# Storing the attention keys from the feature-major tile element by element, in place of turning them to token rows on TensorE

## The chip, the cores and the metric

One core of a Trainium2 chip runs the whole step in one launch. The time is that of the device, in microseconds (us); lower is better. The kernel before has a median of 3550.0 us over 2 runs (3547.46 and 3552.54).

## The reference, cut to what matters

The step pushes two groups of tokens through two layers: a prompt of 16 + 512 = 528 tokens and a sample of 32 tokens, 560 columns in all. Layer 0 is a gated DeltaNet. After it one shared set of keys, values and forget gates is made, and layer 1 is a forgetting attention with 16 heads of 128 features, over the prompt's own keys and, for the sample, over 1024 cached keys and its own 32. The part that the change touches is this:

```
k = rms_norm((rms_norm(h, kv_norm_g) @ kv_w)[..., :2048].reshape(B, L, 16, 128), k_norm_g)
...
return (y_prompt, y_sample, ..., k_p (1, 528, 16, 128), v_p, logf_p, ..., k_s (1, 32, 16, 128), v_s, logf_s)
```

The normed keys are used in the attention and are outputs too: `k_p` and `k_s` are laid out by token, then head, then feature, in float32. The 128 features of one token and head are 512 bytes in a row; the next token's row of the same head lies 16 * 128 * 4 = 8192 bytes further.

## The kernel before, in words

Three stages run one after the other: the DeltaNet layer (up to about 2200 us), the attention layer (`attention_layer`) and an output layer. Activations are kept feature-major: a tile has 128 features on the partitions and the 560 tokens along the free dimension. In the attention stage a **turn** handles two heads at once: in front, the projections of head p (four tiles: key, value, query, gate; each of 2 x 8 `kstep`s of six 280-column matmuls, L1860), and behind them the attention of head p - 1. There are 17 turns: turn 0 has only the front, turns 1 to 15 have both, and the last turn (16) has the last head's attention beside a part of the output projection.

What stands where in a turn is written out by hand in `HEAD_PLACES` (L1602) and `LAST_HEAD_PLACES`: each step has a place among the 64 ksteps, and every engine walks the same list and runs its own part of each step in that order. A step that waits holds up all that stands behind it on its engine. The steps that matter here, with their places:

- `tab` at 2.01: VectorE writes the head's normed keys `kT` and queries `qT` (L2207), both [128 features, 560 tokens], and then `fq`. These three raise `kq_made`. There is one `kT`, so `tab` of the next turn overwrites it, and L2205 makes VectorE wait until the key transposes of the turn before are done (`k_turned`).
- `score` 0 at 11.01: TensorE's first matmul of the attention; it waits for `kq_made`. The splits that make each weight half tile ready (VectorE L2137 and L2142, ScalarE L1988) stand between these steps; `split` at 2.02 is just behind `tab`. TensorE can be two half tiles (16 ksteps) ahead of them.
- `kout` at 64.01, the turn's end: TensorE turns `kT` to token rows with six transposes into the PSUM tiles `b_E` (L1899, L1902), ScalarE copies them to `kn` and `kn2` (L2047, L2049) and issues three stores on its DMA queue (L2053 to L2055). In the last turn `kout` stands at 2.01.
- `put` at 64.03: ScalarE stores the head's attention output `fo` on the same queue.

SyncE loads the weight halves (L1821) into a ring of four. At the end of the stage ScalarE waits for all key and value stores (L2098, L2099).

Other transfers that the rows below name, with the length of one contiguous run: `cl_rows` (L1441) and `wf` (L1439) are loaded in runs of 16 float32, 64 bytes, 1024 and 2048 of them; `TTs` (L780) in 1280 runs of 128 bytes; `M` (L762) is stored in DRAM in 320 runs of 128 bytes an issue; `GT` in 32 runs of 2560 bytes; the log gates (L2011, L2012) in 512 and in 16 runs of 64 bytes; weight halves in 1024 runs of 512 bytes.

Of the kernel before, what the change touches and what calls it, by code (L numbers as in the profile page):

```python
# [22 lines left out]
P = 128  # L23
# [4 lines left out]
PROMPT = N_META + SEQ  # L28
SAMPLE = 32
NTOK = PROMPT + SAMPLE  # L30
# [25 lines left out]
FH = 16  # L56
# [138 lines left out]
def wait(engine, point):  # L195

    if point is not None:
        engine.wait_ge(*point)
# [1480 lines left out]
def attention_layer(nc, top, io, keep, scratch):  # L1679
# [4 lines left out]
    with ExitStack() as ctx:  # L1684
        def sb(name, shape, dt=F32):
            return ctx.enter_context(nc.sbuf_tensor("b_" + name, shape, dt))
# [4 lines left out]
        def signal(name, kind, per=1):  # L1691
            return Signal(sem(name), kind, per)

        main = [ctx.enter_context(nc.psum_tensor(f"b_main{i}", [P, 512], F32)) for i in range(4)]
        E = [ctx.enter_context(nc.psum_tensor(f"b_E{i}", [P, 512], F32)) for i in range(2)]
        F = keep["F"]
# [4 lines left out]
        raw = sb("raw", [P, 3, NTOK])  # L1701
        sq, root, rr = sb("sq", [P, NTOK]), sb("root", [P, NTOK]), sb("rr", [P, 2, NTOK])
        kT, qT = sb("kT", [P, NTOK]), sb("qT", [P, NTOK])
        zt, znew, zs = sb("zt", [P, NTOK]), sb("znew", [P, NTOK]), sb("zs", [P, NTOK])
        kn, vn = sb("kn", [P, 4, P]), sb("vn", [P, 4, P])
        kn2, vn2 = sb("kn2", [SAMPLE, 2, P]), sb("vn2", [SAMPLE, 2, P])
        kc, vc = sb("kc", [P, PAST // P, P]), sb("vc", [P, PAST // P, P])
        kcT = sb("kcT", [P, PAST])
        fbp, fbs = sb("fbp", [P, PROMPT]), sb("fbs", [SAMPLE, PAST + SAMPLE])
# [20 lines left out]
        sumsq = signal("sumsq", "sumsq")  # L1730
        rooted, inverted = signal("rooted", "root"), signal("inverted", "recip")
        moved = signal("moved", "tab")
        kq_made = signal("kq_made", "tab", 3)
        k_turned, k_took, k_out = signal("k_turned", "kout"), signal("k_took", "kout"), signal("k_out", "kout", 48)
        v_turned, v_took, v_out = signal("v_turned", "vout"), signal("v_took", "vout"), signal("v_out", "vout", 48)
        kc_in, vc_in = signal("kc_in", "fetchk", 16), signal("vc_in", "fetch", 16)
        fb_in = signal("fb_in", "fetch", 32)
        kc_turned, kc_took = signal("kc_turned", "kcache"), signal("kc_took", "kcache")
# [5 lines left out]
        fo_out = signal("fo_out", "put", 16)  # L1744

        bank_e = [
            Bank({"kout": (lambda: True, k_took), "kcache": (lambda: True, kc_took), "sumsq": (lambda t: True, rooted),
                  "turn": (lambda i: True, pt_made)}),
            Bank({"kout": (lambda: True, k_took), "kcache": (lambda: True, kc_took), "sumsq": (lambda t: True, rooted),
                  "value": (lambda i: True, gated), "score": (lambda i: i == 5, biased)}),  # L1750
        ]
        bank_f = [
            Bank({"vout": (lambda: True, v_took), "score": (lambda i: i % 2 == 0 or i >= 4, biased)}),
            Bank({"vout": (lambda: True, v_took), "score": (lambda i: i % 2 == 1 or i >= 4, biased)}),
        ]
# [70 lines left out]
        def _(pe):  # L1826

            def body(turn):
                p = turn.p
                for step in turn.steps():  # L1830
# [18 lines left out]
                    elif what == "kstep":  # L1849
                        n, k = a  # L1850
                        t = n // 2
# [14 lines left out]
                    elif what == "gates":  # L1866
# [10 lines left out]
                        elif n == 4:  # L1877
                            pe.wait_ge(g_v, 7)
                            for i in range(BLOCKS):
                                nc.tensor.transpose(E[0][0:QN[i], FH * i:FH * i + FH], lf[3][:, Q0[i]:Q0[i] + QN[i]], ident[0:FH, 0:FH])  # L1880
                                src = fp[:, Q0[i]:Q0[i] + QN[i]] if i < 5 else fs[:, PAST:PAST + SAMPLE]
                                m = nc.tensor.transpose(E[1][0:QN[i], FH * i:FH * i + FH], src, ident[0:FH, 0:FH])
                            m.then_inc(g_p, 1)
                    elif what == "sumsq":
                        t, = a
# [4 lines left out]
                            wait(pe, bank_e[e].free(turn, step))  # L1890
                            m = nc.tensor.matmul(E[e][:, 0:HALF], ones[:, :], sq[:, e * HALF:(e + 1) * HALF], start=True, stop=True)
                        m.then_inc(sumsq.sem, 1)
                    elif what in ("kout", "vout"):
                        src, b, guards, sig = ((kT[:], E, bank_e, k_turned) if what == "kout" else (raw[:, 1], F, bank_f, v_turned))
                        wait(pe, kq_made.after(turn))
                        for g in guards:
                            wait(pe, g.free(turn, step))
# [23 lines left out]
                    elif what == "turn":  # L1921
# [4 lines left out]
                        for j in range(nb):  # L1926
                            n = tail if j == nb - 1 else P
                            out, src = E[0][0:n, QN[i] * j:QN[i] * j + QN[i]], pr[0:QN[i], i % 2, P * j:P * j + n]
# [27 lines left out]
        def _(act):  # L1956
            kp, ks = (io[n].rearrange("b t h d -> (b t) h d") for n in ("k_p", "k_s"))
            vp, vs = (io[n].rearrange("b t h d -> (b t) h d") for n in ("v_p", "v_s"))
            cache_k, cache_v = (io[n].rearrange("b (c p) h d -> p (b c) h d", p=P) for n in ("cache_k", "cache_v"))

            def body(turn):
                p = turn.p
                again = not (turn.fixed and p == 1)
                for step in turn.steps():
                    what, *a = step
                    if what == "o_split":
                        k, = a
                        if k < FH - 1:
                            act.wait_ge(o_in[k % O_RING], 16 * (k // O_RING + 1))
                            src = o_raw[:, k % O_RING]  # L1970
                        else:
                            wait(act, gated.after(turn, 5))
                            src = fo[:]
# [40 lines left out]
                    elif what == "evac":  # L2014
                        t, = a
# [10 lines left out]
                    elif what == "root":  # L2026
                        t, = a
# [6 lines left out]
                    elif what == "tab":  # L2034
# [1 line left out]
                            wait(act, gated.after(turn, 5, ago=1))  # L2036
                        wait(act, gate.after(turn, ago=1))
                        nc.scalar.activation(zs[:], znew[:], ACT.Copy).then_inc(moved.sem, 1)
                    elif what in ("kout", "vout"):
                        turned, took, out, b, rows, rows2, dst, dst2 = (  # L2040
                            (k_turned, k_took, k_out, E, kn, kn2, kp, ks) if what == "kout" else
                            (v_turned, v_took, v_out, F, vn, vn2, vp, vs))
                        wait(act, turned.after(turn))
                        if again:
                            wait(act, out.after(turn, ago=1))
# [6 lines left out]
                        h = bass.ds(p - 1, 1)  # L2052
# [42 lines left out]
                        wait(act, gated.after(turn, 5))  # L2095
                        act.dma_start(scratch["fo"][bass.ds(p - 1, 1)].rearrange("k p t -> p (k t)"), fo[:]).then_inc(fo_out.sem, 16)
            turns(act, body)
            act.wait_ge(k_out.sem, 48 * FH)  # L2098
            act.wait_ge(v_out.sem, 48 * FH)  # L2099
            act.wait_ge(fo_out.sem, 16 * (FH - 1))  # L2100
            act.wait_ge(stored, 5 * 16)
# [2 lines left out]
        def _(dve):  # L2104
            def body(turn):
                p = turn.p
                again = not (turn.fixed and p == 1)
                for step in turn.steps():
# [68 lines left out]
                    elif what == "evac":  # L2177
                        t, = a
                        dve.wait_ge(sub_used, SUBS_B * p + 2 * t + 2)
                        b = main[2 * (t % 2):2 * (t % 2) + 2]  # L2180
# [4 lines left out]
                        out = znew if t == 3 else raw[:, t]  # L2185
# [15 lines left out]
                    elif what == "tab":  # L2201
                        wait(dve, inverted.after(turn, 2, 1, ago=1))
                        if again:
                            wait(dve, scored.after(turn, 5, ago=1))
                            wait(dve, k_turned.after(turn, ago=1))  # L2205
                        for out, t, g in ((kT, 0, 49), (qT, 2, 50)):
                            nc.vector.scalar_tensor_tensor(out=out[:], in0=raw[:, t], scalar=vec[:, g:g + 1], in1=rr[:, t // 2],  # L2207
                                                           op0=ALU.mult, op1=ALU.mult).then_inc(kq_made.sem, 1)
# [239 lines left out]
```

## Time and profile before

| | |
|---|---|
| median of 2 runs | 3550.0 us |
| profiled execution, its own time | 3539.89 us |
| its span, first to last instruction | 3538.0 us |
| mean granted TensorE clock | 0.976 |
| TensorE matmuls busy | 3393.7 us (96%) |
| VectorE / ScalarE busy | 2160.1 us (61%) / 1466.1 us (41%) |
| DMA packets, bytes | 689799, 375.75 MB |

A row of the page gives, for one engine, the busy time and its share of the span; the digits show the span in 40 slices of 88 us. Rows of the timeline give start, length, engine, line, what is written and read, and in brackets the idle time ahead of it with what ended it.

### The profile page before, as it was taken

The page shows a single profiled execution, that of the slowest core. Times are in us where ns is not written, and L with a number is a line of the kernel's source. Part 1 is how long each engine was busy: PE and PEld are TensorE (multiplying, and loading weights), DVE is VectorE, ACT ScalarE, POOL GpSimd, SP SyncE. Part 2 cuts the span into 40 slices and gives each one's busy share as a digit, 9 for nine tenths or more (in the row PEclk, how much of TensorE's full clock was granted, in tenths as well). Part 3 has the DMA queues.
Part 4 walks back from the last instruction along what each step waited for, and adds up shares of the span by engine and source line. Part 5 has one row for each costly group of instructions (what it writes and reads, how often), then busy time and mean ns, then how long its engine had stood idle before and what let it go on. Part 6 is the DMA issues. An engine that isn't in the chain of part 4 may idle for free. (4 is left out here: it accounts for less than half of the span.)

```text
span 3538.0 us, 68787 instructions
## 1 busy us (share of the span) xinstructions
PE 3393.7 (96%) x25217; PEld 3249.8 (92%) x25217; DVE 2160.1 (61%) x3614; ACT 1466.1 (41%) x3062; POOL 794.1 (22%) x1058
## 2 busy tenths in 40 slices
PE   4989999999999999999889999999999999999799
PEld 2989999999999999999889998999899999999799
DVE  5656766777766767767533234766666666666522
ACT  4345545555555555555422222333333333333312
POOL 2333555544444555344400000000000000000000
PEclk7999999999999999999899999999999999999999
DMA  4423344343433343333545433333333333333343
GB/s 145 107 73 98 107 104 115 92 109 80 111 104 98 104 115 90 89 101 98 152 121 164 129 118 101 98 98 97 97 85 103 88 97 96 96 97 107 115 136 111
DMA packets 689799, 375.75 MB, mean 106 GB/s; under 512 B 135443, under 2 KB 654470, under 8 KB 689126
## 3 DMA queue, kind: packets, MB, share of 16 engines
q1 hardware_dynamic: 591958, 303.36, 31.6%
q10 hardware_dynamic: 97728, 70.81, 6.7%
q8 instruction: 80, 1.31, 0.2%
q14 instruction: 33, 0.27, 0.0%
HBM read 297.98 MB, written 55.15 MB: 100 GB/s over the span
## 5 line engine op out<-in xcount | busy, mean ns | idle before, releaser
L933 PE MATMUL main<-xh,w_hi 128*128 128x280 f32 x3072 | 712.5, 313 | 14.2 <-DVE w_lo L1206 14.2
L933 PE MATMUL main<-xh,w_lo 128*128 128x280 f32 x3072 | 651.6, 293 | 0.0
L933 PE MATMUL main<-xl,w_hi 128*128 128x280 f32 x3072 | 648.9, 293 | 0.0
L933 PEld LDWEIGHTS main<-xh,w_hi 128*128 128x128 f32 x3072 | 496.5, 191 | 26.4 <-issue 15.1
L933 PEld LDWEIGHTS main<-xh,w_lo 128*128 128x128 f32 x3072 | 493.0, 190 | 0.0
L933 PEld LDWEIGHTS main<-xl,w_hi 128*128 128x128 f32 x3072 | 490.8, 190 | 0.0
L1860 PE MATMUL b_main<-xh,w_hi 128*128 128x280 f32 x2048 | 471.6, 312 | 0.0
L1860 PE MATMUL b_main<-xh,w_lo 128*128 128x280 f32 x2048 | 432.2, 292 | 0.0
L1860 PE MATMUL b_main<-xl,w_hi 128*128 128x280 f32 x2048 | 431.6, 292 | 0.0
L888 POOL TENSOR_TENSOR prod<-Ml,Tl 40x30 f32<-40x30 f32 (+14 forms) x480 | 330.1, 688 | 37.6
L1860 PEld LDWEIGHTS b_main<-xh,w_hi 128*128 128x128 f32 x2048 | 326.0, 190 | 12.0
L892 POOL TENSOR_TENSOR Tl<-Tl,prod 40x30 f32<-40x30 f32 (+14 forms) x480 | 324.1, 675 | 37.6
L1860 PEld LDWEIGHTS b_main<-xh,w_lo 128*128 128x128 f32 x2048 | 327.3, 190 | 0.0
L1860 PEld LDWEIGHTS b_main<-xl,w_hi 128*128 128x128 f32 x2048 | 326.1, 189 | 0.0
L1206 DVE TENSOR_TENSOR w_lo<-w_raw,w_hi 128x1024 fp32r<-128x1024 f32 x192 | 249.3, 1298 | 62.6 <-ACT w_hi L1053 61.1
L1215 DVE SCALAR_TENSOR_TENSOR y<-xp,cw,y 128x640 f32<-128x640 f32 x192 | 195.3, 1017 | 106.2 <-ACT y L1073 92.0
L2142 DVE TENSOR_TENSOR w_lo<-b_w_raw,w_hi 128x1024 fp32r<-128x1024 f32 x126 | 153.3, 1216 | 136.1 <-ACT w_hi L1988 136.1
L1137 ACT ACTIVATE oq<-F,ptab 64x128 f32<-64x128 f32 x288 | 104.4, 362 | 314.6 <-DVE Rr L1324 218.0
L1053 ACT ACTIVATE w_hi<-w_raw 128x1024 fp32r<-128x1024 f32 x192 | 202.2, 1053 | 76.5 <-PE main L933 65.3
L1547 DVE TENSOR_TENSOR w_lo<-a_w_raw,w_hi 128x1024 fp32r<-128x1024 f32 x56 | 68.6, 1225 | 232.2 <-ACT w_hi L1513 232.2
L860 POOL TENSOR_TENSOR W<-Mc,const_all 32x256 f32<-32x256 f32 x32 | 34.6, 1081 | 728.4 <-DVE QKc L1302 727.1
L2081 ACT ACTIVATE b_pr<-b_pr,b_stat 128x128 f32<-128x128 f32 (+2 forms) x96 | 66.6, 693 | 289.3 <-DVE b_stat L2231 289.3
(314 smaller groups left out, 6327.9 us busy)
## 6 DMA issues: line engine op xcount, KB each, us to landing
w_raw<-in_a_w_in SPq DMA_DIRECT2D x192, 512.0 KB, 4.4
b_w_raw<-in_b_w_in SPq DMA_DIRECT2D x64, 512.0 KB, 4.1
b_w_raw<-in_kv_w SPq DMA_DIRECT2D x62, 512.0 KB, 4.2
a_w_raw<-in_a_w_out SPq DMA_DIRECT2D x54, 512.0 KB, 4.3
y_w_raw<-in_b_w_out SPq DMA_DIRECT2D x24, 512.0 KB, 4.2
kqk<-kq SPq DMA_DIRECT2D x16, 640.0 KB, 4.1
o<-ot ACTq DMA_DIRECT2D x16, 560.0 KB, 5.8
b_kc<-in_cache_k ACTq DMA_DIRECT2D x16, 512.0 KB, 4.2
```

The costliest lines, as they stand in the source:

```text
L860: return nc.gpsimd.tensor_tensor(out, src, one.broadcast_to(list(src.shape)), ALU.mult)
L888: nc.gpsimd.tensor_tensor(pr, Ml[:, j, j + 1:SUB, None].broadcast_to([LANES, below, across]), Tl[:, j:j + 1, 0:across].broadcast_to([LANES ...
L892: nc.gpsimd.tensor_tensor(Tl[:, j + 1:SUB, 0:across], Tl[:, j + 1:SUB, 0:across], pr, ALU.subtract).then_inc(chained.sem, 1)
L933: m = nc.tensor.matmul(main[2 * (t % 2) + h][:, 0:HALF], hi[:, n % SPLIT_RING, k, :], x[:, KSUB * (n % 2) + k, h * HALF:(h + 1) * HALF], s ...
L1053: nc.scalar.activation(w_hi[:, n % SPLIT_RING], w_raw[:, n % RAW_RING], ACT.Copy).then_inc(hi_made, 1)
L1137: m = nc.scalar.activation(oq[r], F[0][r, HD * (1 - h):HD * (2 - h)], ACT.Copy, scale=ptab[r, 40 + c:41 + c])
L1206: nc.vector.tensor_tensor(w_lo[:, n % SPLIT_RING], w_raw[:, n % RAW_RING], w_hi[:, n % SPLIT_RING].bitcast(F32), ALU.subtract).then_inc(lo ...
L1215: nc.vector.scalar_tensor_tensor(out=y[:], in0=x, scalar=weight, in1=y[:], op0=ALU.mult, op1=ALU.add).then_inc(taps.sem, 1)
L1547: nc.vector.tensor_tensor(w_lo[:, g % split_ring], w_raw[:, g % raw_ring], w_hi[:, g % split_ring].bitcast(F32), ALU.subtract).then_inc(lo ...
L1860: m = nc.tensor.matmul(main[2 * (t % 2) + e][:, 0:HALF], hi[:, n % split_ring, k, :], x[:, KSUB * (n % 2) + k, e * HALF:(e + 1) * HALF], s ...
L2081: nc.scalar.activation(pr[q, i % 2, 0:KN[i]], pr[q, i % 2, 0:KN[i]], ACT.Exp, bias=stat[q, i % 2, 1:2], accum_out=stat[q, i % 2, 2:3]).the ...
L2142: nc.vector.tensor_tensor(w_lo[:, n % split_ring], w_raw[:, n % raw_ring], w_hi[:, n % split_ring].bitcast(F32), ALU.subtract).then_inc(lo ...
```

## The change

The keys no longer go through TensorE, PSUM and ScalarE. At the same place in the turn ScalarE issues two stores that read `kT` as it lies, feature by feature, and write each element to its place in `k_p` or `k_s`. `kn` and `kn2` are gone, the PSUM tiles `b_E` have one user less, and `tab` of the next turn waits for these stores' completion (`k_out`) where it waited for the transposes.

```diff
-        kn, vn = sb("kn", [P, 4, P]), sb("vn", [P, 4, P])
-        kn2, vn2 = sb("kn2", [SAMPLE, 2, P]), sb("vn2", [SAMPLE, 2, P])
+        vn, vn2 = sb("vn", [P, 4, P]), sb("vn2", [SAMPLE, 2, P])
...
-        k_turned, k_took, k_out = signal("k_turned", "kout"), signal("k_took", "kout"), signal("k_out", "kout", 48)
+        k_out = signal("k_out", "kout", 32)
...
 # TensorE
-                    elif what in ("kout", "vout"):
-                        src, b, guards, sig = ((kT[:], E, bank_e, k_turned) if what == "kout" else (raw[:, 1], F, bank_f, v_turned))
+                    elif what == "vout":
+                        src, b, guards, sig = raw[:, 1], F, bank_f, v_turned
...
 # ScalarE
-                    elif what in ("kout", "vout"):
-                        turned, took, out, b, rows, rows2, dst, dst2 = (
-                            (k_turned, k_took, k_out, E, kn, kn2, kp, ks) if what == "kout" else
-                            (v_turned, v_took, v_out, F, vn, vn2, vp, vs))
+                    elif what == "kout":
+                        wait(act, kq_made.after(turn))
+                        h = bass.ds(p - 1, 1)
+                        act.dma_start(kp[:, h, :].rearrange("t h d -> d (t h)"), kT[:, 0:PROMPT], allow_slow_non_contiguous=True).then_inc(k_out.sem, 16)
+                        act.dma_start(ks[:, h, :].rearrange("t h d -> d (t h)"), kT[:, PROMPT:NTOK], allow_slow_non_contiguous=True).then_inc(k_out.sem, 16)
+                    elif what == "vout":
+                        turned, took, out, b, rows, rows2, dst, dst2 = v_turned, v_took, v_out, F, vn, vn2, vp, vs
...
-            act.wait_ge(k_out.sem, 48 * FH)
+            act.wait_ge(k_out.sem, 32 * FH)
...
 # VectorE, step tab
-                            wait(dve, k_turned.after(turn, ago=1))
+                            wait(dve, k_out.after(turn, ago=1))
```

On ScalarE, at the end of a turn and the start of the next, before: `b_zt` is the gate's tanh, `b_kn` the key rows, `fo` the attention output in DRAM, `b_zs` the first work of the next turn.

```order
L2025 ACTIVATE b_zt<-b_znew 128x560
L1986 REGISTER_ALU
L1988 ACTIVATE w_hi<-b_w_raw 128x1024
L2047 ACTIVATE b_kn<-b_E 128x512
L2049 ACTIVATE b_kn<-b_E 16x128
L2049 ACTIVATE b_kn<-b_E 32x128
L2053 DMA out_k_p<-b_kn 128x4x128
L2054 DMA out_k_p<-b_kn 16x128
L2055 DMA out_k_s<-b_kn 32x128
L2096 ISA
L2096 DMA fo<-b_fo 128x560
```

The same place in the change:

```order
L2024 ACTIVATE b_zt<-b_znew 128x560
L1985 REGISTER_ALU
L1987 ACTIVATE w_hi<-b_w_raw 128x1024
L198 ISA
L2041 DMA out_k_p<-b_kT 128x528x1
L2042 DMA out_k_s<-b_kT 128x32x1
L2098 ISA
L2098 DMA fo<-b_fo 128x560
L1767 REGISTER_ALU
L1767 COMPARE_AND_BRANCH
L2037 ACTIVATE b_zs<-b_znew 128x560
```

Three copies and a store are gone, and the two stores left have a last dimension of one element; their place ahead of `fo` and of the next turn is the same.

On TensorE, at the end of the same turn, before (`b_main` rows are the projections):

```order
L1860 MATMUL b_main<-xh,w_lo 128x280 x2
L1899 MATMUL b_E<-const_all,b_kT 128x128 x4
L1902 MATMUL b_E<-const_all,b_kT 16x128
L1902 MATMUL b_E<-const_all,b_kT 32x128
L1768 REGISTER_ALU
L1768 COMPARE_AND_BRANCH
L1860 MATMUL b_main<-xh,w_hi 128x280 x2
```

And in the change:

```order
L1859 MATMUL b_main<-xh,w_lo 128x280 x2
L1767 REGISTER_ALU
L1767 COMPARE_AND_BRANCH
L1859 MATMUL b_main<-xh,w_hi 128x280 x2
L1859 MATMUL b_main<-xl,w_hi 128x280 x2
```

The six transposes are gone, and the projections of one turn run straight into those of the next.

## Rows read from the trace of the kernel before

**Rows 1.** The page: TensorE's busy time; its granted clock in 40 slices.

```profile
PE 3393.7 (96%) x25217; PEld 3249.8 (92%) x25217; DVE 2160.1 (61%) x3614; ACT 1466.1 (41%) x3062; POOL 794.1 (22%) x1058
...
PEclk7999999999999999999899999999999999999999
```

**Rows 2.** Busy us in a stretch of the attention stage; then clock, DMA share, GB/s.

```profile
2310.00:3310.00 1000.00, 980.18 (x7228) 916.50 (x7228) 664.21 (x1104) 355.42 (x669) 0.00 (x0) 0.99 0.35 99
```

**Rows 3.** Timeline of ScalarE where one turn ends.

```profile
2389.07 1.04 ACT L1988 ACTIVATE w_hi<-b_w_raw 128x1024 fp32r<-128x1024 f32 x1
2390.02 0.58 ACT L2047 ACTIVATE b_kn<-b_E 128x512 f32<-128x512 f32 x1
...
2390.93 0.41 ACTq L2053 DMA_DIRECT2D out_k_p<-b_kn  x1
...
2392.54 0.36 ACTq L2096 DMA_DIRECT2D fo<-b_fo  x1
```

**Rows 4.** Timeline of VectorE there.

```profile
2391.95 0.79 DVE L2207 SCALAR_TENSOR_TENSOR b_kT<-b_raw,vec,b_rr 128x560 f32<-128x560 f32 x1
2392.66 0.79 DVE L2207 SCALAR_TENSOR_TENSOR b_qT<-b_raw,vec,b_rr 128x560 f32<-128x560 f32 x1
2393.37 0.16 DVE L2211 COPY b_fq<-fcol 128x6 f32 x1
```

**Rows 5.** Timeline of TensorE there, without the projections.

```profile
2386.37 0.60 PE L1899 MATMUL b_E<-const_all,b_kT 128*128 128x128 f32 x4
2386.80 0.38 PE L1902 MATMUL b_E<-const_all,b_kT 128*16 128x128 f32 x2
...
2396.58 0.38 PE L1919 MATMUL b_F<-b_kT,b_qT 128*128 128x128 f32 x2
```

**Rows 6.** Line L2053: register moves of the 13 looped turns, first and last start.

```profile
L2053 ACTq MOVE out_k_p<-b_kn x13: 29/29/29, 2388.8 to 3215.3; - x13
```

**Rows 7.** DMA view: a queue's packets, MB, share; then issues, KB each, us to landing.

```profile
q1 hardware_dynamic: 591958, 303.36, 31.6%
...
out_k_p<-b_kn ACTq DMA_DIRECT2D x16, 256.0 KB, 2.6
...
M<-Mc SPq DMA_DIRECT2D x64, 40.0 KB, 1.7
...
TTs<-T SPq DMA_DIRECT2D x16, 160.0 KB, 2.9
...
G<-GT SPq DMA_DIRECT2D x1, 80.0 KB, 1.7
...
out_logf_p<-b_lf_rows ACTq DMA_DIRECT2D x1, 32.0 KB, 4.5
...
out_logf_p<-b_lf_rows ACTq DMA_DIRECT2D x1, 1.0 KB, 4.1
```

**Rows 8.** Timeline of SyncE: the issue of 2048 runs of 64 bytes.

```profile
1821.68 1.75 SPq L1439 DMA_DIRECT2D a_wf<-in_kv_w  x1
```

**Rows 9.** Stretches as in rows 2: half a us of 64-byte runs.

```profile
1826.50:1827.00 0.50, 0.50 (x6) 0.50 (x6) 0.00 (x0) 0.50 (x1) 0.00 (x0) 1.00 1.67 144
```

**Rows 10.** Stretches as in rows 2: an idle TensorE and what follows.

```profile
1810.00:1815.00 5.00, 0.00 (x1) 0.00 (x0) 1.94 (x3) 1.06 (x1) 0.00 (x0) 1.00 0.48 167
1815.00:1820.00 5.00, 2.41 (x10) 2.44 (x11) 0.19 (x2) 0.00 (x0) 0.00 (x0) 0.52 0.20 55
1820.00:1825.00 5.00, 5.00 (x34) 5.00 (x33) 0.00 (x0) 0.00 (x0) 0.00 (x0) 0.80 1.16 303
```

**Rows 11.** Timeline of the last turn: the key copy, and VectorE's last work.

```profile
3309.15 0.60 ACT L2047 ACTIVATE b_kn<-b_E 128x512 f32<-128x512 f32 x1 [0.35 <-PE b_E L1902]
...
3359.09 0.73 DVE L2115 TENSOR_TENSOR xl<-b_fo,xh 128x560 fp32r<-128x560 f32 x1
```

More of the change, by code:

```diff
@@ L1746, in attention_layer @@
         bank_e = [
-            Bank({"kout": (lambda: True, k_took), "kcache": (lambda: True, kc_took), "sumsq": (lambda t: True, rooted),
+            Bank({"kcache": (lambda: True, kc_took), "sumsq": (lambda t: True, rooted),
                   "turn": (lambda i: True, pt_made)}),
-            Bank({"kout": (lambda: True, k_took), "kcache": (lambda: True, kc_took), "sumsq": (lambda t: True, rooted),
+            Bank({"kcache": (lambda: True, kc_took), "sumsq": (lambda t: True, rooted),
                   "value": (lambda i: True, gated), "score": (lambda i: i == 5, biased)}),
```

## The prediction, made before the changed kernel ran

> **What bounds the kernel now.** I read the page first: TensorE is busy for 96% of the span, and its clock digits are 9 nearly everywhere [rows 1]. Then the stretch of the attention stage that the change touches: of 1000 us TensorE works 980 at a clock of 0.99, VectorE 664, ScalarE 355, and the DMA engines are 0.35 busy [rows 2]. So any time in which TensorE stands still adds to the total, and work taken from ScalarE or VectorE is worth nothing by itself. Third, the timelines where one turn ends and the next begins, to see how close the key store's issue lies to the next write of `kT`: ScalarE issues it at 2390.93 [rows 3], VectorE overwrites `kT` from 2391.95 [rows 4]. One microsecond apart; the present store reads `kn`, not `kT`, so nobody minds. TensorE needs the new `kT` at 2396.58, for score 0 [rows 5]. The looped turns are (3215.3 - 2388.8) / 12 = 68.9 us long [rows 6].
>
> **What goes.** Six transposes a head, some 0.8 us of TensorE (2386.37 to 2387.18) [rows 5], three ScalarE copies from 2390.02, 0.9 us up to the store's issue [rows 3], and one store. Undisturbed, TensorE's part alone would be worth 16 x 0.8 = 13 us.
>
> **What comes: the store.** A head has 128 x 560 = 71680 elements, and no two neighbours in `kT` are neighbours in DRAM, so I count 71680 runs of 4 bytes, 4480 for each of 16 DMA engines. The queue of the weight loads supports one packet for one contiguous run: 303.36 MB in 591958 packets is 512 bytes a packet [rows 7], the length of a weight run. The present store has 512-byte runs, 528 + 32 of them, and lands in 2.6 us [rows 7].
>
> No row has 4-byte runs of data, so I bound the price of one, over all engines together. The fixed part of a landing is 1.7 us (`GT`, 32 long runs) [rows 7].
> - Low end: in the half microsecond of 64-byte runs the engines move 144 GB/s [rows 9]; 144 / 64 = 2.25 runs a ns, 0.44 ns each. Nothing in the rows is faster, but it is a short load.
> - Middle: `TTs`, 1280 runs of 128 bytes, lands in 2.9 us [rows 7]: (2.9 - 1.7) / 1280 = 0.94 ns each. The issue of `wf`, 2048 runs, holds SyncE's queue for 1.75 us [rows 8], 0.85 ns each.
> - High end: a 4-byte run as dear as a 512-byte one: 0.316 x 16 x 3538 us / 591958 = 30.2 ns on one engine, 1.89 ns over 16 [rows 7].
>
> I take 0.94: it is a whole transfer of short runs, from issue to landing, and lies midway in ratio between the ends. The store then lasts D = 1.7 + 71680 x 0.94 ns = 69.1 us, from 33.2 us (0.44) to 137.2 us (1.89). The log gates' store of 512 runs takes 4.5 us, but 16 runs beside it take 4.1 [rows 7], so that is a shared wait and no price.
>
> A page's price for the same thing: the Trainium skill, "DMA: Bandwidth & Descriptors", section Bandwidth, has about 10.5 ns a packet on one engine in the smallest load it measured; 4480 of these are 47 us, D = 49, and by the sum below an estimate of some 4250 us. No row here shows it for stores of 4 bytes; `TTs` is at 15 ns by the same count [rows 7], and I stay with the row.
>
> **Where it lands.** `kout` stays at the end of the turn, and the next `tab` now waits for the landing. The store can go out when ScalarE reaches it, at about 2390.0, where the first copy stood [rows 3]. VectorE would write `kT` at 2390.0 + D, and `kq_made` is complete 1.6 us later (2391.95 to 2393.53) [rows 4]. TensorE runs on through 11 ksteps and the cached keys' transposes and stops at score 0, which came at 2396.58 [rows 5]. So score 0 is late by 2390.0 + D + 1.6 - 2396.6 = **D - 5.0**; what the transposes gave back only makes TensorE wait earlier. Queued on VectorE behind that wait are the scaling and splitting of the next weight half; TensorE has five ksteps left to cover them when score 0 is through, so I add nothing. On ScalarE's queue `fo` stands behind the store; its reader waits for `value` 0, later still. SyncE's loads have a ring of four and fill it while all stand.
>
> **What the standstill costs beside.** After a stretch of 5 us in which TensorE did nothing the granted clock was 0.52 and 0.80 in two stretches of 5 us with 2.41 and 5.00 us of work [rows 10], one level (1.2 GHz) and then the other (2.4): 2.41 x 0.48 + 5.00 x 0.20 = 2.2 us lost. I take 2.2 for each restart. One turn grows by D - 5.0 + 2.2 = D - 2.8.
>
> **How often.** `tab` waits in turns 2 to 16: 15 times. The 16th store is issued in the last turn at about 3309.2 (copy at 3309.15) and the stage cannot end before it lands; VectorE's last work ends at 3359.8 [rows 11]. It is hidden up to D = 50.6.
>
> **Sum**, against the profiled execution's 3540 us: 15 x (69.1 - 2.8) = 994; last turn 69.1 - 50.6 = 18; together 3540 + 994 + 18 = 4552. The median of the runs shown is 10 us above that execution, so I say **4560 us**. With D = 33.2: 3540 + 15 x 30.4 + 10 = 4006. With D = 137.2: 3540 + 15 x 134.4 + 87 + 10 = 5653.
>
> **Rivals.**
> 1. *Short runs cost the engines only their own beat* (0.44 to 0.6 ns). For it: the 144 GB/s stretch [rows 9]. Against: that is a load of 64-byte runs in a burst too short to show whether issuing them can keep up, and [rows 8] is twice as dear. Time 4000 to about 4180 us.
> 2. *Partial writes to DRAM set the pace.* Sixteen engines at once write neighbouring 4-byte words of the same 512-byte rows; if each costs what a 512-byte run costs, D = 137 and the time is 5650 us, more if they queue for the same row. Against: `M`, stored in 128-byte runs, lands in 1.7 us, no later than `GT` with long runs [rows 7]; but that is 320 runs an issue, 128 bytes each. By the Trainium skill, "DMA: Bandwidth & Descriptors", section Specifications, transfers under 512 bytes make the DMA read, modify and write; the row of `M` does not show a price for it, and no run here shows 4 bytes.
> 3. *Not slower.* The wait at `tab` decides only from D = 5.0 us on, where score 0 would come late. A store that landed by then would leave the 13 us of transposes as a gain: 3527 + 10 = 3537 us. That takes the stores going out in runs longer than an element, or 0.05 ns an element, nine times quicker than the best row [rows 9]. The one-element last dimension of the change's stores speaks against it.
> 4. *The queue holds up the loads.* If 71680 runs block the weight loads of the other queue while they are generated, as SyncE's own queue was held for 1.75 us by 2048 [rows 8], TensorE also waits for weights after each store: two loads of some 4 us each a turn would be 15 x 8 = 120 us on top, 4680 us; inside the forecast's own range.
>
> **How the numbers follow.** The forecast (0.6 to 1.3 ns, 4180 to 4950 us, rival 4 within it) has 0.45; rival 1 has 0.23; rival 2 has 0.30, of it 0.13 beyond 5900 us; rival 3 has 0.01; something faster than 3980 yet slower than now 0.01. The range of 3980 to 5900 leaves out 0.15. A measurement of this kernel tells 2%, 71 us, from no change: slower 0.98, same 0.01, faster 0.01.
>
> **What would show it.** In the changed kernel's profile: the store's row with a landing near 69 us, 16 times; 16 x 71680 = 1.15 million more packets on ScalarE's queue; VectorE's `kT` row with an idle time of about D - 2 ended by the DMA, 15 times; TensorE idle ahead of score 0 by about D - 4, and the clock digits of the attention stage below 9; head turns of 135 us in place of 68.9. The prediction is wrong in size if the landing differs, and wrong in kind if the landing is long but `tab` does not wait for it, or if TensorE stops elsewhere than at score 0.

## The result, and the profile after

The changed kernel takes **7130.3 us** (median of 2 runs, 7116.18 and 7144.39) against 3550.0 before: a ratio of 2.01, interval 2.004 to 2.016. The forecast of 4560 us had the direction right, and the chain of events up to the last turn, and the size wrong; 7130 lies above its range. The profiled execution takes 7116.18 us, 3576.3 more than that of before.

The page: busy time by engine, the granted clock in 40 slices, and ScalarE's DMA queue (packets, MB, share of 16 engines' span); then the same queue on the page before.

```profile
PE 3421.6 (48%) x25121; PEld 3273.9 (46%) x25121; DVE 2164.4 (30%) x3614; ACT 1454.2 (20%) x3014; POOL 793.9 (11%) x1058
...
PEclk8999999999999575765656656566575665656569
...
q10 hardware_dynamic: 1235392, 70.81, 72.2%
```

```profile
q10 hardware_dynamic: 97728, 70.81, 6.7%
```

TensorE's work is that of [rows 1], in twice the span. The digits 5 to 7 begin where the attention stage begins. The queue carries the same 70.81 MB as before, in 1.24 million packets in place of 97,728. So the bytes are not what is new on it; whether the number of packets is the load, or what each of them does, this page does not tell.

Who waits, in us in total, times, and the longest:

```profile
PE b_F L1918 <- DVE b_fq L2213: 3218.7, 15, 232.7
DVE b_kT L2209 <- DMA out_k_s<-b_kT: 3171.3, 14, 234.9
ACT b_zs L2037 <- issue: 2074.5, 14, 154.6
```

VectorE waits at `tab` for the store, 3171.3 / 14 = 226.5 us each time, and TensorE waits for `fq` ahead of score 0. These two waits are one stall seen twice, and must not be added. The timelines of one turn's end answer to [rows 3, 4]. ScalarE:

```profile
2911.72 0.69 ACTq L2041 DMA_DIRECT2D out_k_p<-b_kT  x1
2912.50 134.99 ACTq L2042 DMA_DIRECT2D out_k_s<-b_kT  x1
3047.65 16.42 ACTq L2098 DMA_DIRECT2D fo<-b_fo  x1
3064.62 0.67 ACT L2037 ACTIVATE b_zs<-b_znew 128x560 f32<-128x560 f32 x1 [151.57 <-issue]
```

And VectorE:

```profile
3146.20 0.80 DVE L2209 SCALAR_TENSOR_TENSOR b_kT<-b_raw,vec,b_rr 128x560 f32<-128x560 f32 x1 [231.24 <-DMA out_k_s<-b_kT]
```

From the issue at 2911.72 to the new `kT` at 3146.20 it is 234.5 us: this is the forecast's D, for this turn. It is the idle time of 231.24 plus 3.3, so the mean D is 226.5 + 3.3 = **229.8 us**, where 69.1 was forecast. The first store's issue returns after 0.69 us; the second is held for 135 us, and ScalarE with it.

Stretches of the stall before that one (2622 to 2847 us) and after it, read as [rows 2, 10]:

```profile
2640.00:2660.00 20.00, 0.00 (x0) 0.00 (x0) 0.00 (x0) 0.00 (x0) 0.00 (x0) 0.50 1.79 29
2820.00:2847.00 27.00, 0.00 (x0) 0.00 (x0) 0.00 (x0) 0.00 (x0) 0.00 (x0) 0.50 0.22 6
2847.00:2867.00 20.00, 18.04 (x118) 16.85 (x118) 16.00 (x33) 5.41 (x14) 0.00 (x0) 0.87 0.23 67
2867.00:2890.00 23.00, 22.22 (x157) 19.55 (x158) 17.20 (x32) 8.90 (x16) 0.00 (x0) 1.00 0.26 70
```

In the first two stretches every compute engine stands still and the clock is at its lower level (0.50 of full speed, 1.2 GHz). When TensorE starts again it gets 0.87 over 18.04 us of work, a loss of 18.04 x 0.13 = 2.3 us (2.2 forecast), and then full clock. So the low digits of the page are in the main the stall's consequence. The DMA share tells something too. Packets overlap on the engines, so that it reads 1.79 early in the stall; in the last 27 us it is 0.22, and still the store has not landed. Few packets are under way at the end of the stall; what the store still waits for then, this view does not show.

The last turn, ScalarE:

```profile
6681.67 1.06 ACT L1980 ACTIVATE w_hi<-b_w_raw 128x1024 fp32r<-128x1024 f32 x1 [82.70 <-DMA b_w_raw<-in_b_w_out]
...
6689.26 126.10 ACTq L2042 DMA_DIRECT2D out_k_s<-b_kT  x1
...
6815.46 1.06 ACT L1980 ACTIVATE w_hi<-b_w_raw 128x1024 fp32r<-128x1024 f32 x1 [125.49 <-issue]
...
6910.91 1.06 ACT L1980 ACTIVATE w_hi<-b_w_raw 128x1024 fp32r<-128x1024 f32 x1 [53.78 <-DMA b_w_raw<-in_b_w_out]
```

Here the store stalls the kernel in three other ways. Its issue keeps ScalarE from its next split for 125 us; VectorE stands behind that split, and TensorE behind VectorE:

```profile
6818.94 0.48 PE L1931 MATMUL b_E<-const_all,b_pr 128*128 128x128 f32 x1 [122.18 <-DVE b_pr L2240]
```

The wait of 82.70 us ahead of 6681.67 stands in the place of the 15th wait at `tab`. The weight half that ended it was late because its issue was late. On SyncE's queue it stands behind a load of the attention output `fo`, and that load had to wait for `fo`'s store. SyncE's own wait, and its issues:

```profile
SPq L1797 <- DMA fo<-b_fo: 67.3, 1, 67.3
```

```profile
6675.60 1.18 SPq L1792 DMA_DIRECT2D b_w_raw<-in_b_w_out  x2
...
6819.36 0.46 SPq L1792 DMA_DIRECT2D b_w_raw<-in_b_w_out  x1
```

`fo`, behind the key store on ScalarE's queue, lands 96.0 us after its issue (median), where it took 4.4 us before. The weight half itself, issued at 6675.60, was there 6 us later. The third way is the wait of 53.78 us: the weight half issued at 6819.36, when by a D of 230 us the last key store was still on its way, was there only at 6910.9, after 91.5 us.

**The whole.** From the first write of `kT` to the last it was 2254.8 to 3303.7, and is 2261.3 to 6684.6: 15 turns, each longer by 225.0 us, 3374 in all. From the last `kT` to the output layer's first matmul it was 58 us (3303.7 to 3361.8) and is 253 (to 6938.0): 195 more. All earlier stages were 6.5 us longer. 3374 + 195 + 6.5 = 3576, the whole difference of the profiled executions. The rows, before and after (nanoseconds of one, then first and last start in us):

```profile
L2207 DVE SCALAR_TENSOR_TENSOR b_kT<-b_raw,vec,b_rr x16: 793/793/797, 2254.8 to 3303.7; 128x560 f32<-128x560 f32 x16
L2328 PE MATMUL y_main<-xh,w_hi x416: 287/291/572, 3361.8 to 3530.9; 128*128 128x280 f32 x139
```

```profile
L2209 DVE SCALAR_TENSOR_TENSOR b_kT<-b_raw,vec,b_rr x16: 795/801/803, 2261.3 to 6684.6; 128x560 f32<-128x560 f32 x16
L2330 PE MATMUL y_main<-xh,w_hi x416: 287/291/570, 6938.0 to 7107.4; 128*128 128x280 f32 x139
```

### The profile page after: what moved, and what is told of

Same layout as the page of the kernel before. It is cut to its first block and busy times, and to the rows that moved or that the text cites. A ratio compares the mean times of both kernels' runs of the same rounds, so it can differ in the third digit from the quotient of the medians.

```text
span 7114.4 us, 68513 instructions
## 1 busy us (share of the span) xinstructions
PE 3421.6 (48%) x25121; PEld 3273.9 (46%) x25121; DVE 2164.4 (30%) x3614; ACT 1454.2 (20%) x3014; POOL 793.9 (11%) x1058
## 3 DMA queue, kind: packets, MB, share of 16 engines
q10 hardware_dynamic: 1235392, 70.81, 72.2%
## 5 line engine op out<-in xcount | busy, mean ns | idle before, releaser
L1918 PE MATMUL b_F<-b_kT,b_qT 128*128 128x128 f32 (+2 forms) x192 | 73.5, 483 | 3218.7 <-DVE b_fq L2213 3218.7
L1918 PEld LDWEIGHTS b_F<-b_kT,b_qT 128*128 128x128 f32 (+1 forms) x192 | 30.8, 194 | 3235.9 <-DVE b_fq L2213 3222.1
L2209 DVE SCALAR_TENSOR_TENSOR b_kT<-b_raw,vec,b_rr 128x560 f32<-128x560 f32 x16 | 12.8, 801 | 3171.3 <-DMA out_k_s<-b_kT 3171.3
L1987 ACT ACTIVATE w_hi<-b_w_raw 128x1024 fp32r<-128x1024 f32 x126 | 132.9, 1055 | 1201.7 <-DVE b_w_raw L2139 1169.5
```

Source lines behind the costliest of these rows:

```text
L1918: m = nc.tensor.matmul(b[0:QN[i], 0:n], qT[:, Q0[i]:Q0[i] + QN[i]], keys, start=True, stop=True)
L1987: nc.scalar.activation(w_hi[:, n % split_ring], w_raw[:, n % raw_ring], ACT.Copy).then_inc(hi_made, 1)
```

## The experiments

The open question was why an element costs 3.2 ns and not 0.94. The theories that the expectations name are these. **A**: the packet itself is dear, wherever it goes. **B**: stores into the same 64 bytes of DRAM hinder one another, because several DMA engines store there (B1) or because the next store comes too soon after the last, whoever sends it (B2). **C**: storing only a part of such a 64-byte line is dear even alone. **Theory D** (not the forecast's D, which is a time): the sample's store is late because of its place in the queue.

Runs 1 to 11 keep the place and the wait. So the mean idle time at `tab`, divided by the number of runs (71680 where both stores go out), is the price of one to within 0.02 ns, and to within 0.4 ns in run 8 with its 4096. Runs 1 to 12 are one execution each; the kernel before took 3540 to 3555 us on their chips. All runs but 4 and 12 to 14 leave key outputs unwritten.

**1. Every element in 64 bytes of its own** in a scratch tensor, tokens 8 KB apart as in the outputs.

```diff
-act.dma_start(kp[:, h, :].rearrange("t h d -> d (t h)"), kT[:, 0:PROMPT], ...)
+act.dma_start(scratch["kd"][0:PROMPT, :, 0].rearrange("t d -> d t"), kT[:, 0:PROMPT], ...)
...
+                   "kd": dram("kd", (NTOK, P, 16))}
```

> Same 71680 four-byte stores a head from the same place, tokens 8192 bytes apart as before, but each element has a 64-byte line of its own in a scratch buffer in DRAM (features 64 bytes apart), so no two stores share a line; the key outputs stay unwritten. In the changed kernel the wait for the store is some 225 us a turn, of it about 140 for the prompt's 67584 elements (2.1 ns each) and 81 for the sample's 4096 (20 ns each). Theory A, the price is that of a packet, whatever it writes: unchanged, 225 us a turn, 7100 us. Theory B, stores of several engines into one line queue for each other: the price falls to that of the short runs in the kernel before, 0.44 to 0.94 ns, 33 to 69 us a turn, 4000 to 4600 us. Theory C, a store of part of a line is dear even alone: the sample falls to the prompt's price, some 150 us a turn, 5900 us.

5186.6 us. The wait fell to 1467.4 / 14 = 104.8 us, less than half. Its wait, and the second issue here and in the change (min, median and max in ns):

```profile
DVE b_kT L2209 <- DMA kd<-b_kT: 1467.4, 14, 108.7
```

```profile
L2042 ACTq DMA_DIRECT2D kd<-b_kT x16: 92119/97172/101697, 2323.1 to 4863.1; - x16
```

```profile
L2042 ACTq DMA_DIRECT2D out_k_s<-b_kT x16: 126103/131936/136393, 2327.3 to 6689.3; - x16
```

The second issue is held 97 us here (median), so with D = 104.8 + 3.3 all has landed some 10 us after it, while in the change it is held 132 us (median) and all has landed some 97 us after it (229.8 - 0.7 - 132). Same number of packets, same bytes: theory A does not explain the change, and stores that share 64 bytes explain more than half of it. Most of the gain is in the sample's store, 97 us before and 10 here.

**2. The same number of 4-byte runs, loaded** from the cached keys.

```diff
+act.dma_start(kd[:, 0:PROMPT], ck[0:PROMPT, h, :].rearrange("t h d -> d (t h)"), ...)
...
```

> The stores are replaced by loads of as many four-byte elements from the key cache in DRAM, 8192 bytes from token to token as in the key output, into a spare tile; the key outputs stay unwritten. Theory A (price of a packet): 225 us a turn, 7100 us. Theories B and C (writing is what is dear): 33 to 69 us a turn, 4000 to 4600 us.

4338.1 us; wait 713.7 / 14 = 51.0 us, 0.71 ns a run.

```profile
DVE b_kT L2211 <- DMA b_kd<-in_cache_k: 713.7, 14, 51.4
```

**3. 71680 stores of a whole 64 bytes each.**

```diff
+act.dma_start(scratch["kd"][:, 0:PROMPT, :], kT[:, None, 0:16].broadcast_to([P, PROMPT, 16]), ...)
...
```

> As many runs, 71680 a head, but each writes a whole 64-byte line of a scratch buffer (its source is the first 16 columns of the key tile, again and again); the key outputs stay unwritten. Sixteen times the bytes. Theory A (price of a packet): at least 225 us a turn, 7100 us or more. Theories B and C (stores of part of a line): 33 to 69 us a turn, 4000 to 4600 us.

4367.6 us; 731.3 / 14 = 52.2 us, 0.73 ns a run, with 16 times the bytes.

```profile
DVE b_kT L2209 <- DMA kd<-b_kT: 731.3, 14, 52.4
```

So a load of an element, or a store of a whole 64 bytes, costs half of a store of 4 bytes alone in its 64 (1.46).

**4. The sample's store issued ahead of the prompt's.**

```diff
+act.dma_start(ks[:, h, :].rearrange("t h d -> d (t h)"), kT[:, PROMPT:NTOK], ...)
 act.dma_start(kp[:, h, :].rearrange("t h d -> d (t h)"), kT[:, 0:PROMPT], ...)
-act.dma_start(ks[:, h, :].rearrange("t h d -> d (t h)"), kT[:, PROMPT:NTOK], ...)
```

> The changed kernel with the sample's store issued ahead of the prompt's. Theory B (32 token rows give each line's next store too soon): the sample still takes some 80 us, now in front, and the total stays within 3% of 7130 us. A rival, theory D: the sample's store was slow only because it stood behind the prompt's in a full queue; then the wait shrinks by some 75 us a turn, to about 5900 us.

6985.5 us; 3035.0 / 14 = 216.8 us. The order hardly matters, and theory D falls: in front of everything the sample's store still takes 96.6 us from issue to landing (min, median and max).

```profile
DMA to landing us min/median/max: 90.3/96.6/108.0
```

What is held now is the issue that stands third, `fo` (min, median and max in ns):

```profile
L2042 ACTq DMA_DIRECT2D out_k_p<-b_kT x16: 10262/17838/22896, 2319.2 to 6541.3; - x16
...
L2098 ACTq DMA_DIRECT2D fo<-b_fo x15: 186219/197907/211016, 2337.4 to 6315.6; - x15
```

The hold goes with the number of packets that stand ahead: 18 us behind the sample's 4096, 198 us behind all 71680. It does not go with their landing, for the 4096 land only after 96.6 us.

**5. Own 64 bytes, tokens 64 bytes apart** in place of 8 KB.

```diff
+act.dma_start(scratch["kd"][:, 0:PROMPT, 0], kT[:, 0:PROMPT], ...)
...
+                   "kd": dram("kd", (P, NTOK, 16))}
```

> As the run with a 64-byte line for each element, but the lines of one feature lie one behind the other (64 bytes from token to token, not 8192), so that each DMA engine walks through DRAM without large strides; the key outputs stay unwritten. So far: 64-byte runs that fill their line cost 55 us a turn (0.74 ns a run), 4-byte stores into lines of their own at 8192-byte stride 110 us a turn. If the difference is the price of a store that fills only part of a line: again some 110 us a turn, 5190 us. If it is the stride: 55 us a turn, 4370 us.

5408.8 us; 1653.7 / 14 = 118.1 us, 1.65 ns. The 8 KB step between tokens is not the cause. A part of a line costs about twice a whole one (0.73) even when nobody else touches it: theory C holds too.

```profile
DVE b_kT L2209 <- DMA kd<-b_kT: 1653.7, 14, 121.0
```

**6. Eight elements to each 64 bytes, back to back.** The stores are those of run 5, into a narrower tensor.

```diff
+                   "kd": dram("kd", (P, NTOK, 2))}
```

> The elements of one feature lie 8 bytes apart in a scratch buffer, so eight stores share a 64-byte line, but all of them come from one DMA engine, one right behind the other; the key outputs stay unwritten. Theory B1, it is several engines in one line that is dear: as with lines of their own, 110 us a turn or less, at most 5200 us. Theory B2, it is the next store to a line coming too soon after the last, whoever sends it: dearer than the 225 us a turn of the changed kernel, over 7100 us, since here they are back to back. If neighbours in one line are even joined, 55 us a turn, 4370 us.

7933.0 us, slower than the change itself; 276.3 us, 3.85 ns.

```profile
DVE b_kT L2209 <- DMA kd<-b_kT: 3867.5, 14, 285.4
```

Against run 5 only the spacing differs, and the price is 2.3 times as high: stores into the same 64 bytes soon after one another hinder each other. It needs no neighbouring features, since each 64 bytes take one feature's elements alone: B2 holds, and B1 as the whole cause, which expected at most 5200 us, falls.

**7. The prompt's store alone**.

```diff
-act.dma_start(ks[:, h, :].rearrange("t h d -> d (t h)"), kT[:, PROMPT:NTOK], ...)
...
```

> The changed kernel without the sample's store (its key output stays unwritten): 67584 of 71680 elements a head remain. If the sample's 4096 elements cost what the prompt's do, 6% less waiting: about 6900 us. If they take some 80 us of the 225 by themselves, the wait falls to about 145 us a turn: 3540 + 15 x 145 + some 100 in the last turn = 5700 to 5850 us.

5432.4 us; 1681.9 / 14 = 120.1 us, below the 145 us that were expected.

```profile
DVE b_kT L2208 <- DMA out_k_p<-b_kT: 1681.9, 14, 127.0
```

94% of the elements take 53% of the wait, 1.78 ns each; the sample's 4096 elements account for the other 226.5 - 120.1 = 106 us, 26 ns each.

**8. The sample's store alone**, in 4096 elements.

```diff
-act.dma_start(kp[:, h, :].rearrange("t h d -> d (t h)"), kT[:, 0:PROMPT], ...)
...
```

> The changed kernel with the sample's store alone, 4096 elements a head; the prompt's key output stays unwritten. If the 32 rows are dear by themselves: 80 to 105 us a turn, 4800 to 5150 us. If they were dear only behind the prompt's store: at the prompt's price 7 us + 2, a turn longer by some 6 us, 3640 us.

5014.4 us; 1319.0 / 14 = 94.2 us. The DMA view (KB each, median us from issue to landing):

```profile
out_k_s<-b_kT ACTq DMA_DIRECT2D x16, 16.0 KB, 96.1
```

16 KB take 96 us with nothing else on that queue: 23 ns an element. Neither the prompt's packets nor the order is needed for it. It sweeps 32 rows of 512 bytes feature by feature, so it comes back to the same 64 bytes after 32 tokens, where the prompt's store comes back after 528. That this early return is what makes it dear fits runs 1 and 6; no run separates it from the small piece of memory that all its elements share.

**9. Four elements to each 64 bytes** (features 16 bytes apart, rows 8 KB apart).

```diff
+act.dma_start(scratch["kd"][0:PROMPT, 0:512].rearrange("t (d f) -> d t f", f=4)[:, :, 0], kT[:, 0:PROMPT], ...)
...
```

> 4-byte stores with tokens 8192 bytes apart, features 16 bytes apart in a scratch buffer, so that a 64-byte line takes four neighbouring features, in place of 16 in the key output and 1 in the own-lines run; the key outputs stay unwritten. So far the wait at the key tile is 227 us a turn in the changed kernel (120 without the sample, so 106 for the sample's 4096 elements) and 105 with a line for each element. If it takes many partitions' stores in flight to one line at once to make it dear, and four neighbours go through one engine one token sweep after the other: about 105 us again, 5190 us. If a line that is stored to again within 32 tokens is dear whoever sends it: the sample still takes a quarter of its 106 us or more, 135 us or more a turn, 5650 us or more.

5686.9 us; 1916.2 / 14 = 136.9 us, between own lines (104.8) and the change (226.5). In the same sweep, more sharers of a line take more time.

**10. On-chip, no DRAM**: the same runs from `kT` to a second tile.

```diff
+        kd = sb("kd", [P, NTOK, 2])
...
+act.dma_start(kd[:, 0:PROMPT, 0], kT[:, 0:PROMPT], ...)
...
```

> 71680 four-byte runs a head copied from the key tile into a spare tile on the chip (every second word), so no DRAM at either end; the key outputs stay unwritten. The load from DRAM and the stores of whole lines both waited 51 to 52 us a turn. If that is what a packet costs the queue and the engines: 51 us again, 4340 us. If DRAM has a share in it: less, down to 0.44 ns a run, 31 us a turn, 4000 us. If short writes are dear on the chip's own memory too: 105 us or more, 5190 us.

4208.2 us; 598.9 / 14 = 42.8 us, 0.60 ns a run, 9.6 ns on one of 16 engines.

```profile
DVE b_kT L2210 <- DMA b_kd<-b_kT: 598.9, 14, 42.9
```

This is the floor of theory A: packets alone are 43 of the 227 us. The Trainium skill, "DMA: Bandwidth & Descriptors", section Bandwidth, has about 10.5 ns a packet and does not say over how many engines; read as the price on one engine, as the prediction read it, it is near the 9.6 here and the 0.71 x 16 = 11.4 ns of the load in run 2.

**11. One store over all 560 tokens**, same strides, in a scratch tensor.

```diff
+act.dma_start(scratch["kd"][:, 0:P].rearrange("t d -> d t"), kT[:], ...)
...
```

> One store a head over all 560 tokens into a scratch buffer laid out as the key output (16 features to a 64-byte line, tokens 8192 bytes apart); the key outputs stay unwritten. So far: prompt alone 120 us a turn (1.8 ns an element), prompt and sample in two stores 227 us. If the sample is dear because its 32 rows are swept again and again by themselves, all 71680 elements now cost the prompt's price: 127 us a turn, 5500 us. If the 4096 elements are dear for another reason: still some 220 us, 7000 us.

6412.6 us; 2529.9 / 14 = 180.7 us. Neither expectation holds (127 or 220 us). Taking the sample's rows into the long sweep saves 46 us, as an early return would have it; but 2.52 ns an element is well above the prompt's own 1.78, though the sweep is no shorter. That difference stays open; the store goes to another tensor too, which no run tests by itself.

**12. The store early in the turn**, so that `kT` need not be free for 60 us.

```diff
-        "kout": [64.01],
+        "kout": [2.03],
```

> The changed kernel with the store moved from the end of the turn (64.01) to its start (2.03), right behind the write of the key tile, so that a whole turn lies between it and the next write. Theory: a turn lasts as long as the store, some 228 us in place of 299, and ScalarE, held by the issue for 130 us, still gets its 62 us of work done in it: 3540 + 15 x (228 - 69) + some 20 = 5950 us. Rival: the store makes no way beside the turn's other transfers, and the turn stays near 299 us: 7100 us. That a turn's own work hides it, 3540 us, is excluded by the 225 us.

6493.7 us, between the two expectations (5950 and 7100). A turn takes (6074.2 - 2256.5) / 15 = 254.5 us by its `kT` rows, and nobody waits for the store any more. ScalarE's timeline and the waits:

```profile
3273.23 124.88 ACTq L2042 DMA_DIRECT2D out_k_s<-b_kT  x1
3398.20 1.09 ACT L2063 ACTIVATE b_kcT<-b_E 128x512 f32<-128x512 f32 x2 [126.66 <-issue]
```

```profile
ACT b_kcT L2063 <- issue: 1768.9, 15, 126.7
...
DVE b_w_raw L2139 <- DMA b_w_raw<-in_b_w_in: 786.6, 25, 56.7
```

The wait at `tab` is replaced by ScalarE held in the issue, 1768.9 / 15 = 118 us a turn on average (the row shown is one of the longest), and by weight halves up to 57 us late. Taking away the wait that the profile names gives back 637 of 3580 us; the slow queue then stalls the kernel elsewhere.

**13. The keys turned in 32 x 32 blocks on VectorE**, stored from SyncE's queue in runs of 32 features (128 bytes).

```diff
+nc.vector.transpose(kb[:, 0:17].rearrange("p c j -> p (c j)"), kT[:, 0:544])
+nc.vector.transpose(kb[:, 17], kT[:, PROMPT:NTOK]).then_inc(k_turned.sem, 1)
...
+sp.dma_start(kp[0:512, h, d].rearrange("(c i) h d -> i c (h d)", i=32), kb[r, 0:16]).then_inc(k_out.sem, 16)
...
+        "kout": [22.02],
...
```

> All outputs as in the reference. The keys are turned on VectorE in blocks of 32 by 32 (two transposes a head) and stored in runs of 128 bytes, 2240 a head, by 12 stores on SyncE's queue in the middle of the turn; TensorE's six transposes and ScalarE's copies are gone, as in the change. By the price per run (0.94 ns as of 128-byte runs before) a store lasts some 4 us and has a whole turn to land. TensorE bounds the stage, so its 0.8 us a head come back: 16 x 0.8 = 13 us, ratio 0.9965. Rivals: VectorE pays some 0.8 us a head for it at a place where TensorE waits for it, no change, ratio 1.000; or the 12 issues, 5 us of SyncE's queue, delay the weight loads, up to 5 us a turn, ratio 1.02.

3534.5 us against 3540.3 before on the same chip: ratio 0.9987, interval 0.9972 to 1.0001: no change clear of the noise. The two transposes, then TensorE's wait beside them from 2310 to 3290 us, here and in the kernel before:

```profile
L2256 DVE STREAM_TRANSPOSE b_kb<-b_kT x16: 736/739/741, 2265.9 to 3309.3; 128x544 f32<-128x544 f32 x16
...
L2257 DVE STREAM_TRANSPOSE b_kb<-b_kT x16: 167/169/173, 2266.6 to 3309.9; 128x32 f32<-128x32 f32 x16
```

```profile
PE b_E L1966 <- DVE b_fo L2266: 18.4, 14, 1.4
```

```profile
PE b_E L1950 <- DVE b_fo L2248: 8.2, 14, 0.7
```

0.9 us of VectorE a head is cheap, but it stood just ahead of work for which TensorE waits: that wait was 8.2 us in the kernel before and is 18.4. By these rows 10 of the 13 us that the six transposes took are lost again here.

**14. The same, with the transposes at another place** (kstep 38) and the stores behind the next turn's second weight load.

```diff
-        "kout": [22.02],
+        "kout": [38.01],
...
+                    store_keys(turn, ago=1)
...
```

> The version with 32 by 32 blocks on VectorE and 128-byte runs, with the two transposes at kstep 38, where VectorE was idle, in place of 22, just ahead of value 0, where TensorE's waits had risen from 8.2 to 18.4 us in the stretch; the stores go out behind the second weight load of the next turn. All outputs as in the reference. If that wait was what was lost: another 10 us, 3525 us, ratio 0.996. If not: as the run before, 0.9987.

3534.1 us against 3548.3 before: ratio 0.9961, interval 0.9947 to 0.9975: 0.4% less than the kernel before, small but clear of the noise, with all outputs written. TensorE's wait and the store's landing:

```profile
PE b_E L1967 <- DVE b_fo L2267: 8.4, 14, 0.6
```

```profile
out_k_p<-b_kb SPq DMA_DIRECT2D x64, 64.0 KB, 1.8
```

The wait is back at 8.4 us, and 0.0039 x 3548 = 14 us are gained, about the 13 us of TensorE's transposes [rows 5]. The stores moved along with the transposes, and the intervals of runs 13 and 14 overlap a little; that the place of the transposes made the difference rests on the two wait rows.

The prices side by side, by the idle time at `tab`:

| stores of one head | wait, us | ns a run |
|---|---|---|
| on-chip, 4 bytes | 42.8 | 0.60 |
| load from DRAM, 4 bytes | 51.0 | 0.71 |
| whole 64 bytes to DRAM | 52.2 | 0.73 |
| 4 bytes alone in 64, two spacings | 104.8, 118.1 | 1.46, 1.65 |
| 16 to each 64 bytes, prompt only | 120.1 | 1.78 |
| 4 to each 64 bytes, both stores | 136.9 | 1.91 |
| 16 to each, 560 tokens in one store | 180.7 | 2.52 |
| the change | 226.5 | 3.16 |
| 8 to each, back to back | 276.3 | 3.85 |
| sample only | 94.2 | 23.0 |

## Why the prediction was wrong in size

- **What goes**: right. Six transposes a head are 13 us of TensorE, and run 14 gives them back where their replacement stands clear of TensorE's waits.
- **Count of runs and where it lands**: right. 1.14 million more packets on ScalarE's queue (1.15 forecast); the wait at `tab`; TensorE stopped at score 0 and nowhere else in a looped turn. Its idle time there is 224.3 us on average without the last one of 78.2, which is D - 5.5 (D - 4 forecast). A turn grew by 225.0 us, where D - 2.8 gives 227.0. So the sum with the D that was measured is 15 x 227 = 3405 for the looped part, against 3374; with the last turn's own term, D - 50.6 = 179, and the 10 us it comes to 3540 + 3405 + 179 + 10 = 7134, against 7130.3. That it is as near as that is in part luck, as the last turn below shows.
- **The step that failed** is "I take 0.94 [...] The store then lasts D = 1.7 + 71680 x 0.94 ns = 69.1 us": D was 229.8. Of the miss of 2570 us, 15 x (229.8 - 69.1) = 2410 lie in this term. The packet price behind it was no error: 0.60 on-chip and 0.71 to 0.73 for loads and whole 64 bytes are below 0.94. But that price is of a load of 128-byte runs (`TTs`), and it was put on stores of 4 bytes. What no row of such loads, nor the 128-byte stores of `M`, could tell is the price of storing 4 bytes of a line: 1.46 ns alone, 3.16 in the change, 3.85 and more with neighbours stored soon after one another.
- **The high end** of 1.89 ns was no upper bound. It held that a 4-byte run costs at most what a 512-byte run costs, and took that from the queue of the weight loads; but a 512-byte run fills its lines and has them for itself, and runs 2 and 3 show that a load, or a store of whole 64 bytes, is no measure for a store of 4. Rival 2 named the mechanism ("more if they queue for the same row") and priced it at 5650 us. (The forecast's band of 0.6 to 1.3 ns has a small slip: by its own sum 1.3 ns is 4976 us, not 4950.) By the Trainium skill, "DMA: Bandwidth & Descriptors", section Specifications, transfers under 512 bytes make the DMA read, modify and write: a 4-byte store at twice the price of a whole 64 bytes fits that, though no row shows the read; for whole 64 bytes (0.73 ns) the runs show little or no penalty over a load (0.71).
- **One price for both stores** was the second mistake inside this term. The sample's 6% of the elements make 106 of the 226.5 us (run 7), and 94 alone (run 8). With the prompt's wait alone the time is 5432 us, inside the range.
- **The last turn**: 18 us forecast, 195 measured. With the measured D the forecast's term gives 179, so most of this miss is D again; but the path was another, and that the sizes come near is luck. The forecast hid the store behind the last head's work and did not see that the issue itself holds ScalarE, 126 us. [rows 8] shows the like, 1.75 us for 2048 runs on SyncE; rival 4 took it from there for the loads, and not for the engine that issues. The forecast also let the reader of `fo` wait "later still", where SyncE waited 67.3 us for `fo` in the last turn, with weight halves behind it. Rival 4's late loads are real in one case there (91.5 us from issue to use) and in run 12 (up to 57 us late); in the looped turns no such wait shows.
- **Not slower** (rival 3): excluded, as forecast.

**What stays open**: why one store over 560 tokens is dearer per element than the prompt's store of 528; and what in the memory makes stores to the same 64 bytes slow one another. The runs show that it depends on how many share them and how soon they follow, not where it happens. The unit of 64 bytes was not varied either: 64 bytes are enough for a whole store to be cheap, but no run tried whole pieces of 32, or elements 128 bytes apart.

## What to carry to other kernels

Count the runs of a transfer, price loads and stores apart, and for stores ask whether a run fills whole 64-byte pieces; if many small stores return to the same few rows, no price from longer runs is an upper bound. A store of tens of thousands of runs also holds the engine that issues the next transfer on that queue, so moving the wait was no cure here (run 12). To turn a tile cheaply, use an engine with slack, go for runs of 128 bytes, and put the work where the bound engine is not about to wait for that engine: by the wait rows 10 of 13 us hung on that place.

## What the runs showed of the hardware

- In stores of some 70,000 runs a 4-byte store to DRAM costs 1.5 to 3.9 ns over 16 engines, by what shares its 64 bytes, against 0.7 for a 4-byte load and 0.6 on-chip.
- 4096 elements into 32 rows of 512 bytes took 96 us, 23 ns each; in own 64 bytes, 67584 and 4096 together took about 108.
- With 67584 runs ahead on its queue, the issue of the next transfer held ScalarE 126 to 136 us in the change; with only the sample's 4096 ahead it was 18 us (median of run 4).
- Behind the key store on the same queue, `fo` landed 96.0 us after its issue (4.4 before), and a weight half on SyncE's queue took 91.5 us in the last turn, where the median of that turn's eight is 6.5.
- VectorE turns 128 x 544 float32 in 32 x 32 blocks in 0.74 us, and 512 runs of 128 bytes land in 1.8 us.
